# Transposes and gathers of the first experts moved between gate/up and down, with more PSUM banks

## The chip, the cores and the metric

One core of one Trainium2 chip runs the kernel. The metric is the time of one launch on the device in microseconds (us); a kernel's time is the median of its runs. All data are float32.

## The reference, cut to what matters

One step of a hybrid diffusion backbone: 128 context tokens and 256 latent tokens of width 2048 pass a mixer (attention and a long convolution), then a mixture of 16 SwiGLU experts. Only the experts matter here:

```python
aff = softmax(xs @ w_router)
g, idx = top_k(aff.T, cap)              # cap: 16 context and 32 latent tokens for each expert
xe = xs[idx]                            # gather
a, u = xe @ w_exp_gate, xe @ w_exp_up   # 2048 -> 1024 each
ye = (silu(a) * u) @ w_exp_down * g     # 1024 -> 2048
out = zeros.at[idx].add(ye)             # scatter
```

## The kernel before, in words

**The ring of weights.** Each expert reads 24 pieces of 1024 KB: 16 of gate and up (alternately, each with two channel tiles of 128), then 8 of down. They go through eight places of SBUF (`pieces`), loaded by SyncE's queue (lines 344 to 350). A place is asked for again when TensorE has released the piece in it (`piece_used`): gate/up pieces in pairs after each of the first seven iterations, down pieces one by one. The last two down pieces are asked for when gate/up is over (`gu_done`). The first piece of the next expert needs the first down piece of this one to be used.

**TensorE, one expert** (`expert`, line 818). Eight iterations `i` of gate/up wait for two pieces each and do eight matmuls of 48 slots by 512 columns (line 849; float32 shows two records for a matmul, so 16 in the trace). Then ScalarE takes the SiLU (line 1144), VectorE the product (line 1696), in two halves `n`; TensorE transposes each half (lines 869 to 871), VectorE copies it to `hTe` (line 1700), and eight steps `k` of down follow (line 898), ended by ScalarE's copies to `ye` (line 1148). Every second expert (2, 4, ...) also scatters the pair before it (line 815) beside gate/up and in the gap before down, into banks 4 to 6, which VectorE adds to `facc` (line 1691, semaphore `e_acc`).

**Gathering.** The gather is a matmul with a one-hot selection. For experts 0 to 5, `gather(k)` runs inside expert 0, one channel tile `k` ahead of its use. For experts 6 to 15, `gather_rest(k)` (lines 782 to 791: two matmuls of 320 columns and one of 160, all in bank 7) runs once in each of the eight iterations of experts 1 (`k` 0 to 7) and 3 (`k` 8 to 15). ScalarE copies each tile out of PSUM with the modulation (`gathered_rest`, lines 1119 to 1125, semaphore `gat2_a`). With one bank, tile `k` waits for the copy of tile `k-1`. In ScalarE's program these eight copies come ahead of the expert's two SiLUs.

**Scatter matrices.** `scatter_matrices(t)` (line 797) transposes eight tiles of `selG` for token tile `t` into banks 5 and 6; ScalarE copies them to `scat` (line 1130, semaphore `sg_cp`). All three run in expert 1, after the gathers of iterations 3, 5 and 6. GpSimd copies the inputs of the next expert (`next_inputs`, line 1216) at the end of gate/up, and after expert 1's the first scatter matrix, and clears `facc`.

The order on every engine is written out by hand; nothing is planned at build time.

Of the kernel before, what the change touches and what calls it, by code (L numbers as in the profile page):

```python
# [19 lines left out]
ACT = mybir.ActivationFunctionType  # L20
# [3 lines left out]
P = 128  # L24
D = 2048
KT = D // P
# [12 lines left out]
NE = 16  # L39
# [29 lines left out]
def paired(k):  # L69

    return slice(2 * P * (k // 2) + k % 2, 2 * P * (k // 2 + 1), 2)


def build(nc, x_prompt, x_sample, cache_k, cache_v, cols, w_ada, w_in, qk_g, w_attn_o, f1_w, f_vec, f2_w,
# [3 lines left out]
    with ctx:  # L78
# [286 lines left out]
        def _(pe):  # L365
# [416 lines left out]
            def gather_rest(k):  # L782

                if k == 0:
                    pe.wait_ge(sel2_ready, 3)
                else:
                    pe.wait_ge(gat2_a, k)
                kk, n = paired(k), NE2 * CAPL
                for t in range(2):
                    mm(bank(7, n), res[:, 1 + t, kk], selL[:, t, NE1:NE, :], start=t == 0, stop=t == 1)  # L790
                mm(bank(7, NE2 * CAPC, n), res[:, 0, kk], sel2C, start=True, stop=True).then_inc(gat2, 1)

            pe.wait_ge(sel_ready, 3)
            gather(0)
# [2 lines left out]
            def scatter_matrices(t):  # L797

                for n in (2 * t, 2 * t + 1):
                    pe.wait_ge(sg_ready, t + 1)  # L800
                    if n >= 2:
                        pe.wait_ge(sg_cp, n - 1)
                    for j in range(4):
                        last = trp(bank(5 + n % 2, P, j * P), selG[:, t, n % 2 * 4 + j, :], ident)
                    last.then_inc(sg_tr, 1)

            def scatter(pair, i, m, t):
# [10 lines left out]
            def expert(e, pair=None, first=False, final=False, rest=None):  # L818

                def beside(t):  # L820
                    if pair is not None:
                        scatter(pair, t // MT, t % MT, t)
                    if final and t < 4:
                        broadcast_gates(2 * t, 2, ones2, diag2_ready, g2_bc, g2_used)

                def landing(q):
                    pe.wait_ge(piece_in[q % 8], e * 48 + 16 * (q // 8 + 1))

                if not first:
                    pe.wait_ge(xe_st, e)  # L830
                if pair is not None:
                    pe.wait_ge(sc_st, pair + 1)
                if final:

                    pe.wait_ge(e_yc, 2 * e)
                for i in range(KT // 2):

                    landing(2 * i)
                    landing(2 * i + 1)
                    for k in range(2):  # L840
                        kk = 2 * i + k
                        if first:
                            if kk + 2 < KT:
                                gather(kk + 2)
                            pe.wait_ge(gat_lv, kk + 1)
                            pe.wait_ge(gat_ca, kk + 1)
                        for n in range(2):
                            for u in range(2):
                                last = mm(bank(n, p0=64 * u, p1=64 * u + SLOTS),  # L849
                                          xeT[:, kk, 0, :] if first else x_cur[:, kk, :],  # L850
                                          pieces[:, (2 * i + u) % 8, k * FF + n * NC_:k * FF + (n + 1) * NC_],
                                          start=kk == 0, stop=kk == KT - 1)
                            if kk == KT - 1:
                                last.then_inc(gu_done, 1)
                    if i < KT // 2 - 1:
                        last.then_inc(piece_used, 2)
                    if i % 2 == 1:
                        beside(i // 2)
                    if rest is not None:
                        gather_rest(rest + i)  # L860
                        if rest == 0 and i in (3, 5, 6):
                            scatter_matrices((3, 5, 6).index(i))
                if final:
                    pe.wait_ge(g2_used, 8)
                beside(4)
                for n in range(2):
                    pe.wait_ge(e_h, e * 2 + (n + 1))
                    for j in range(4):
                        o, src, i_ = bank(2 + n, SLOTS, j * SLOTS), h_s[0:SLOTS, n, j * P:(j + 1) * P], \
                            ident[0:SLOTS, 0:SLOTS]  # L870
                        last = mm(o, src, i_, start=True, stop=True) if j == 0 else trp(o, src, i_)
                    last.then_inc(e_htr, 1)
                beside(5)
                pe.wait_ge(e_hT, e * 2 + 1)
                if final:
                    for i in range(2):
                        for q in range(4):
                            landing(16 + 4 * i + q)
                            if i == 0 and q == 2:
                                pe.wait_ge(e_hT, e * 2 + 2)  # L880
                            if i == 1 and q == 2:

                                pe.wait_ge(sc_st, NE // 2)
                                for m in range(MT):
                                    scatter(NE // 2 - 1, 0, m, m)
                            for k in range(2):
                                for u in range(2):
                                    last = mm(bank(2 + i, p0=64 * u, p1=64 * u + SLOTS), hTe[:, 2 * q + k, :],
                                              pieces[:, 4 * i + q, k * FF + u * NC_:k * FF + (u + 1) * NC_],
                                              start=q == 0 and k == 0, stop=q == 3 and k == 1)  # L890
                        last.then_inc(down_done, 1)
                    return
                pe.wait_ge(e_hT, e * 2 + 2)
                for k in range(HK):
                    landing(16 + k)
                    for i in range(2):
                        for u in range(2):
                            last = mm(bank(2 + i, p0=64 * u, p1=64 * u + SLOTS), hTe[:, k, :],  # L898
                                      pieces[:, k, (2 * i + u) * NC_:(2 * i + u + 1) * NC_],
                                      start=k == 0, stop=k == HK - 1)  # L900
                        if k == HK - 1:
                            last.then_inc(down_done, 1)
                    if k < HK - 1:
                        last.then_inc(piece_used, 1)
# [2 lines left out]
            expert(1, rest=0)  # L907
            expert(2, pair=0)
            expert(3, rest=8)
            with pe.Fori(2, NE // 2 - 1) as p:  # L910
                expert(p * 2, pair=p - 1)
                expert(p * 2 + 1)
# [7 lines left out]
        def _(act):  # L920
# [197 lines left out]

            def gathered_rest(k):
                act.wait_ge(gat2, k + 1)  # L1120
                A(xeT[:, k, NE1:NE, 0:CAPL], bank(7, NE2 * CAPL).rearrange("p (e s) -> p e s", e=NE2),
                  ACT.Identity, bias=mod[:, SHIFT2 * KT + k, 1:2], scale=amp[:, 1, k, 1:2])
                A(xeT[:, k, NE1:NE, CAPL:SLOTS],
                  bank(7, NE2 * CAPC, NE2 * CAPL).rearrange("p (e s) -> p e s", e=NE2),
                  ACT.Identity, bias=mod[:, SHIFT2 * KT + k, 0:1], scale=amp[:, 1, k, 0:1]).then_inc(gat2_a, 1)

            def scatter_matrices(t):
                for n in (2 * t, 2 * t + 1):
                    act.wait_ge(sg_tr, n + 1)
                    A(scat[:, n % 2 * 4:n % 2 * 4 + 4, t * P:(t + 1) * P],  # L1130
                      bank(5 + n % 2).rearrange("p (j t) -> p j t", j=4), ACT.Copy).then_inc(sg_cp, 1)

            def expert(e, odd, rest=None):
                if rest is not None:
                    for i in range(8):
                        gathered_rest(rest + i)
                        if rest == 0 and i in (3, 5, 6):
                            scatter_matrices((3, 5, 6).index(i))
                for n in range(2):
                    act.wait_ge(gu_done, e * 2 + (n + 1))  # L1140

                    if n:
                        act.wait_ge(e_h, e * 2 + 1)
                    A(act_s[0:SLOTS, :], bank(n, p1=SLOTS), ACT.Silu).then_inc(e_silu, 1)  # L1144
                for i in range(2):
                    act.wait_ge(down_done, e * 2 + (i + 1))
                    for u in range(2):
# [4 lines left out]
            for k in range(KT):  # L1152
                gathered(k)
            act.wait_ge(ye_zero, 1)
            expert(0, 0)
            expert(1, 1, rest=0)
            expert(2, 0)
            expert(3, 1, rest=8)
# [697 lines left out]
```

## Time and profile before

| what | us |
|---|---|
| median of 3 runs | 2590.87 (2588.39 to 2595.32) |
| the profiled execution, whole | 2595.64 |
| its span, first to last instruction | 2593.7 |
| TensorE busy | 2409.6 (93%) |
| VectorE, ScalarE busy | 436.9, 236.9 |

The experts begin at 1596 us of the span: expert 0's down at 1644, expert 1's at 1710, expert 2's at 1771, expert 3's at 1831; the last expert's gate/up ends at 2539.5. Ahead of 1596 lie the mixer and the routing, which the change doesn't touch. Idle time of an engine costs nothing where another sets the pace, so the stretches are to be read one by one, with the DMA's rate beside TensorE's.

### The profile page before, as it was taken

To read this page: it belongs to the slowest core of one execution; us is meant where nothing else is said; L and a number is where in the kernel's file an instruction comes from. 1 tells how busy PE (TensorE), PEld (TensorE's weight loads), DVE (VectorE), ACT (ScalarE), POOL (GpSimd) and SP (SyncE) were. 2 spreads that over 40 slices of the span, in tenths; PEclk is the share of its full clock that TensorE was granted. 3 is DMA by queue.
4 is the path that set the end of the run, shared out by engine and by line. 5 is a ranking of instruction groups with operands and counts; after the bars stand their busy time and mean duration, and the time that the engine had idled before them with its cause. 6 is when DMAs were issued, how large, how long until landed. Compare 5 with 4: busy or idle time off the path is not lost.

```text
span 2593.7 us, 22327 instructions
## 1 busy us (share of the span) xinstructions
PE 2409.6 (93%) x8986; PEld 1132.3 (44%) x8986; DVE 436.9 (17%) x942; ACT 236.9 (9%) x486; POOL 46.0 (2%) x50
## 2 busy tenths in 40 slices
PE   5899999999999999999999997999989887979896
PEld 2355554444466666555554444333322222222222
DVE  4301111323122111000001204001011010101024
ACT  1100001000021111000000002111000000000001
POOL 0000000000000000000000000000000000000000
PEclk8899999999999999999999998999999999999998
DMA  9964454445423122524442223999999999999995
GB/s 362 352 235 167 174 189 155 147 157 198 162 65 98 65 98 76 200 101 159 162 162 99 97 97 136 388 386 415 416 421 422 422 422 422 422 422 421 422 421 209
DMA packets 196650, 644.87 MB, mean 249 GB/s; under 512 B 8423, under 2 KB 57992, under 8 KB 147112
## 3 DMA queue, kind: packets, MB, share of 16 engines
q1 hardware_dynamic: 194312, 635.55, 63.3%
q10 hardware_dynamic: 2208, 8.24, 0.9%
q8 instruction: 51, 0.84, 0.1%
q0 software_dynamic: 64, 0.13, 0.0%
q14 instruction: 15, 0.12, 0.0%
HBM read 640.21 MB, written 3.67 MB: 248 GB/s over the span
## 4 chain that ended last, share of the span: by engine, by line
PE 76%; DMA 19%; DVE 2%; ACT 1%; issue 1%; SPq 1%; DVEq 0%; ACTq 0%; POOL 0%; POOLq 0%
DMA ring<-in_w_up 14%; PE PS L652 13%; PE PS L404 10%; PE PS L419 10%; PE PS L849 8%; PE PS L898 7%; PE PS L687 6%; PE PS L746 6%; PE PS L671 3%; PE PS L378 3%; DMA ring<-in_w_down 2%; DMA ring<-in_w_ada 2%; PE PS L815 1%; PE PS L642 1%; PE PS L790 1%
## 5 line engine op out<-in xcount | busy, mean ns | idle before, releaser
L849 PE MATMUL PS<-ring,RF 128*48 128x512 f32 x1920 | 442.3, 605 | 77.1 <-DMA ring<-in_w_up 75.3
L652 PE MATMUL PS<-RB,ring 128*128 128x384 f32 x1024 | 336.2, 487 | 0.6 <-ACT RE L1047 0.6
L849 PEld LDWEIGHTS PS<-ring,RF 128*48 128x48 f32 x1920 | 132.3, 124 | 372.2 <-issue 371.7
L652 PEld LDWEIGHTS PS<-RB,ring 128*128 128x128 f32 x1024 | 193.9, 190 | 137.9 <-issue 3.4
L404 PE MATMUL PS<-RB,ring 128*128 128x384 f32 x768 | 251.2, 490 | 1.9 <-DMA ring<-in_w_in 1.9
L419 PE MATMUL PS<-ring,RB 128*128 128x512 f32 x576 | 252.4, 593 | 0.0
L898 PE MATMUL PS<-ring,RF 128*48 128x512 f32 x960 | 223.0, 622 | 6.9 <-DVE RF L1700 4.7
L404 PEld LDWEIGHTS PS<-RB,ring 128*128 128x128 f32 x768 | 146.4, 191 | 109.0 <-issue 9.6
L746 PE MATMUL PS<-ring,RC 128*128 128x512 f32 x384 | 169.2, 601 | 5.2 <-DVE RE L1573 4.7
L419 PEld LDWEIGHTS PS<-ring,RB 128*128 128x128 f32 x576 | 108.1, 190 | 132.1 <-issue 131.8
L898 PEld LDWEIGHTS PS<-ring,RF 128*48 128x48 f32 x960 | 64.2, 129 | 161.3 <-issue 149.0
L1691 DVE TENSOR_TENSOR RC<-RC,PS 128x512 f32<-128x512 f32 x96 | 64.3, 685 | 387.7 <-PE PS L815 387.5
L687 PE MATMUL PS<-RE,ring 128*128 128x384 f32 x384 | 126.5, 486 | 0.0
L746 PEld LDWEIGHTS PS<-ring,RC 128*128 128x128 f32 x384 | 73.7, 193 | 97.9 <-issue 97.3
L378 PE MATMUL PS<-ring,RG 128*32 128x512 f32 x768 | 92.9, 626 | 10.3 <-DMA ring<-in_w_ada 10.3
L815 PE MATMUL PS<-RB,RF 112*128 112x512 f32 x192 | 97.3, 632 | 4.3 <-DVE RC L1691 3.0
L687 PEld LDWEIGHTS PS<-RE,ring 128*128 128x128 f32 x384 | 73.0, 190 | 50.9
L1696 DVE TENSOR_TENSOR RG<-RF,PS 48x512 f32<-48x512 f32 x32 | 22.1, 690 | 389.8 <-ACT RF L1144 389.5
L671 PE MATMUL PS<-RE,ring 128*128 128x384 f32 x256 | 85.2, 486 | 0.0
L1347 DVE SCALAR_TENSOR_TENSOR RE<-PS,KC,RE 128x127 f32 (+1 forms) x96 | 35.5, 412 | 247.3 <-ACT RE L971 242.9
L1144 ACT ACTIVATE RF<-PS 48x512 f32<-48x512 f32 x32 | 18.9, 591 | 509.2 <-PE PS L849 472.8
L1148 ACT ACTIVATE RB<-PS 48x512 f32<-48x512 f32 x64 | 37.9, 592 | 280.3 <-PE PS L898 256.4
(241 smaller groups left out, 1313.7 us busy)
## 6 DMA issues: line engine op xcount, KB each, us to landing
ring<-in_w_gate SPq DMA_DIRECT2D x128, 1024.0 KB, 12.3
ring<-in_w_up SPq DMA_DIRECT2D x128, 1024.0 KB, 14.0
ring<-in_w_down SPq DMA_DIRECT2D x128, 1024.0 KB, 13.4
ring<-in_w_ada SPq DMA_DIRECT2D x48, 2048.0 KB, 13.2
ring<-in_w_in SPq DMA_DIRECT2D x40, 2048.0 KB, 8.1
ring<-in_w_attn_o SPq DMA_DIRECT2D x8, 2048.0 KB, 8.3
ring<-in_w_out SPq DMA_DIRECT2D x8, 2048.0 KB, 8.6
ring<-in_w_hy_o SPq DMA_DIRECT2D x4, 2048.0 KB, 8.0
```

The source lines that it names most:

```text
L378: last = mm(bank(rows_bank, p0=32 * g, p1=32 * g + 32), condS[:, kk, :], ring[:, j0 + h, k, :], start=kk < 4, stop=kk >= KT - 4)
L404: last = mm(bank(c, T), ring[:, 2 + h, k, c * P:(c + 1) * P], hT[:, h * HK + k, :], start=(h == 0 and k == 0), stop=(h == 1 and k == HK - 1))
L419: last = mm(bank(b0 + m), lhs[:, h * HK + k, m * P:(m + 1) * P], ring[:, (n + h) % 4, k, :], start=(h == 0 and k == 0), stop=(h == 1 and k ...
L652: last = mm(bank(F0, T), wide[:, n % 4, k, t % 2 * P:(t % 2 + 1) * P], hT[:, k, :], start=k == 0, stop=k == KT - 1)
L671: last = mm(bank(F1, T), ring[:, (n + 2) % 4, k, j * P:(j + 1) * P], hyT[:, k, :], start=k == 0, stop=k == HYT - 1)
L687: last = mm(bank(F1, T), wide[:, pa % 4, k, j % 2 * P:(j % 2 + 1) * P], qN[k // 4][:, k % 4, :, :].rearrange("p m d -> p (m d)"), start=k ...
L746: last = mm(bank(3 * (q % 2) + m), mixT[:, h * HK + k, m * P:(m + 1) * P], ring[:, n % 4, k, :], start=(h == 0 and k == 0), stop=(h == 1 a ...
L815: mm(bank(4 + n % 3), s_cur[0:64 + SLOTS, m * P:(m + 1) * P], ye[0:64 + SLOTS, 2 * i + u, :], start=True, stop=True).then_inc(e_sc, 1)
L849: last = mm(bank(n, p0=64 * u, p1=64 * u + SLOTS), xeT[:, kk, 0, :] if first else x_cur[:, kk, :], pieces[:, (2 * i + u) % 8, k * FF + n * ...
L898: last = mm(bank(2 + i, p0=64 * u, p1=64 * u + SLOTS), hTe[:, k, :], pieces[:, k, (2 * i + u) * NC_:(2 * i + u + 1) * NC_], start=k == 0, ...
L1148: last = A(ye[64 * odd:64 * odd + SLOTS, 2 * i + u, :], bank(2 + i, p0=64 * u, p1=64 * u + SLOTS), ACT.Copy)
L1691: tt(facc[:, m, q], facc[:, m, q], bank(4 + n % 3), ALU.add).then_inc(e_acc, 1)
```

## The change: what it does

- The transposes of the three `scatter_matrices` move from expert 1's gate/up to expert 0, between its gate/up and its down: one ahead of the transposes of each half `n`, one behind the last. Their eight-tile groups go through four banks (4 to 7) and no longer two. ScalarE copies them after expert 0's SiLUs.
- `gather_rest` of experts 1 and 3 does five tiles in the iterations 0 to 4; the other three are done between gate/up and down, at the same three places. It uses banks 6 and 7 in turn, and waits for the copy of the tile before the last.
- ScalarE does the SiLUs after five copies, and the last three copies behind them.
- Waits are added: tile 0 for the scatter matrices' copies, tile 8 for the accumulations of the first pair (its bank 6), and one for all gathers ahead of the loop over the later experts.

```diff
@@ gather_rest
                 if k == 0:
                     pe.wait_ge(sel2_ready, 3)
-                else:
-                    pe.wait_ge(gat2_a, k)
-                kk, n = paired(k), NE2 * CAPL
+                    pe.wait_ge(sg_cp, 2 * MT)
+                elif k == 8:
+                    pe.wait_ge(e_acc, 3 + 12)
+                    pe.wait_ge(gat2_a, k - 1)
+                elif k > 1:
+                    pe.wait_ge(gat2_a, k - 1)
+                b, kk, n = 6 + k % 2, paired(k), NE2 * CAPL
                 for t in range(2):
-                    mm(bank(7, n), ...)
-                mm(bank(7, NE2 * CAPC, n), ...).then_inc(gat2, 1)
+                    mm(bank(b, n), ...)
+                mm(bank(b, NE2 * CAPC, n), ...).then_inc(gat2, 1)
@@ scatter_matrices, TensorE
-                    if n >= 2:
-                        pe.wait_ge(sg_cp, n - 1)
+                    if n >= 4:
+                        pe.wait_ge(sg_cp, n - 3)
                     for j in range(4):
-                        last = trp(bank(5 + n % 2, P, j * P), ...)
+                        last = trp(bank(4 + n % 4, P, j * P), ...)
@@ expert, TensorE
+                    if rest is not None and i < 5:
+                        gather_rest(rest + i)
+
+                def between(j):
+                    if first:
+                        scatter_matrices(j)
                     if rest is not None:
-                        gather_rest(rest + i)
-                        if rest == 0 and i in (3, 5, 6):
-                            scatter_matrices((3, 5, 6).index(i))
+                        gather_rest(rest + 5 + j)
+
                 beside(4)
+                between(0)
                 for n in range(2):
                     pe.wait_ge(e_h, e * 2 + (n + 1))
                     ...
                     last.then_inc(e_htr, 1)
+                    between(1 + n)
@@ the experts, TensorE
             expert(3, rest=8)
+            pe.wait_ge(gat2_a, KT)
@@ expert, ScalarE
                 if rest is not None:
-                    for i in range(8):
+                    for i in range(5):
                         gathered_rest(rest + i)
-                        if rest == 0 and i in (3, 5, 6):
-                            scatter_matrices((3, 5, 6).index(i))
                 for n in range(2):
                     ...
                     A(act_s[0:SLOTS, :], bank(n, p1=SLOTS), ACT.Silu).then_inc(e_silu, 1)
+                if first:
+                    for t in range(MT):
+                        scatter_matrices(t)
+                if rest is not None:
+                    for i in range(5, 8):
+                        gathered_rest(rest + i)
```

## Rows read from the trace of the kernel before

**Rows 1.** The page's costliest groups: busy us, mean ns, idle before it, its releaser.
```profile
L849 PE MATMUL PS<-ring,RF 128*48 128x512 f32 x1920 | 442.3, 605 | 77.1 <-DMA ring<-in_w_up 75.3
```
**Rows 2.** Stretches (us from the span's start); the last columns are clock, DMA share, GB/s.
```profile
1644.00:1661.00 17.00, 16.95 (x66) 5.38 (x68) 0.00 (x0) 0.90 (x2) 0.00 (x0) 0.82 0.93 351
...
1710.00:1726.00 16.00, 16.00 (x64) 4.88 (x64) 0.00 (x0) 0.59 (x1) 0.00 (x0) 0.85 0.74 281
...
1770.00:1785.00 15.00, 15.00 (x63) 4.20 (x64) 0.86 (x2) 0.14 (x1) 0.51 (x1) 0.90 0.97 392
...
1832.00:1847.00 15.00, 15.00 (x68) 4.79 (x66) 0.00 (x0) 1.09 (x2) 0.00 (x0) 0.92 0.99 394
...
1860.00:2520.00 660.00, 570.23 (x2378) 180.57 (x2374) 73.94 (x132) 39.05 (x66) 12.37 (x18) 0.98 1.01 422
```
**Rows 3.** SyncE's issues of the first gate piece for experts 1 to 5, some second pieces.
```profile
1647.89 0.34 SPq L344 DMA_DIRECT2D ring<-in_w_gate  x1
1650.64 0.34 SPq L344 DMA_DIRECT2D ring<-in_w_up  x1
...
1713.68 0.33 SPq L344 DMA_DIRECT2D ring<-in_w_gate  x1
...
1773.86 0.33 SPq L344 DMA_DIRECT2D ring<-in_w_gate  x1
...
1834.90 0.33 SPq L344 DMA_DIRECT2D ring<-in_w_gate  x1
...
1892.41 0.33 SPq L344 DMA_DIRECT2D ring<-in_w_gate  x1
```
**Rows 4.** Timeline from gate/up's end to down, expert 0.
```profile
1634.16 5.36 PE L849 MATMUL PS<-ring,RE 128*48 128x512 f32 x24
...
1641.42 0.60 PE L871 MATMUL PS<-KC,RG 48*128 48x48 f32 x5 [1.90 <-DVE RG L1696]
...
1642.82 0.73 PE L871 MATMUL PS<-KC,RG 48*128 48x48 f32 x5 [0.80 <-DVE RG L1696]
...
1644.05 16.86 PE L898 MATMUL PS<-ring,RF 128*48 128x512 f32 x64 [0.49 <-DVE RF L1700]
```
**Rows 5.** The same, expert 1, from its last two iterations on.
```profile
1698.23 1.04 PE L804 MATMUL PS<-KC,RC 128*128 128x128 f32 x8
...
1699.20 3.64 PE L849 MATMUL PS<-ring,RF 128*48 128x512 f32 x16
...
1703.96 0.43 PE L791 MATMUL PS<-KC,RA 128*128 128x160 f32 x2
...
1709.83 16.40 PE L898 MATMUL PS<-ring,RF 128*48 128x512 f32 x64 [0.50 <-DVE RF L1700]
```
**Rows 6.** The same, expert 3.
```profile
1821.34 3.64 PE L849 MATMUL PS<-ring,RF 128*48 128x512 f32 x16
...
1831.32 15.39 PE L898 MATMUL PS<-ring,RF 128*48 128x512 f32 x64 [0.50 <-DVE RF L1700]
```
**Rows 7.** Last iterations of gate/up of experts 2, 4 and 5, downs of 4 and 5.
```profile
1758.92 3.64 PE L849 MATMUL PS<-ring,RF 128*48 128x512 f32 x16 [0.83 <-DMA ring<-in_w_up]
...
1879.12 3.64 PE L849 MATMUL PS<-ring,RF 128*48 128x512 f32 x16 [0.82 <-DMA ring<-in_w_up]
...
1890.29 4.93 PE L898 MATMUL PS<-ring,RF 128*48 128x512 f32 x22
...
1938.81 3.64 PE L849 MATMUL PS<-ring,RF 128*48 128x512 f32 x16 [1.33 <-DMA ring<-in_w_up]
...
1945.65 15.64 PE L898 MATMUL PS<-ring,RF 128*48 128x512 f32 x64 [0.64 <-DVE RF L1700]
```
**Rows 8.** TensorE alone: busy us (records), granted clock, DMA share, GB/s.
```profile
1571.00:1572.00 1.00, 0.06 (x1) 1.00 1.02 434
...
1645.00:1646.00 1.00, 1.00 (x6) 0.50 0.99 418
...
1891.00:1892.00 1.00, 1.00 (x6) 1.00 1.05 434
```

More of the change, by code:

```diff
@@ L785, in gather_rest @@
                     pe.wait_ge(sel2_ready, 3)
-                else:
-                    pe.wait_ge(gat2_a, k)
-                kk, n = paired(k), NE2 * CAPL
+                    pe.wait_ge(sg_cp, 2 * MT)
[5 more added lines that the diff above has]
+                b, kk, n = 6 + k % 2, paired(k), NE2 * CAPL
                 for t in range(2):
-                    mm(bank(7, n), res[:, 1 + t, kk], selL[:, t, NE1:NE, :], start=t == 0, stop=t == 1)
-                mm(bank(7, NE2 * CAPC, n), res[:, 0, kk], sel2C, start=True, stop=True).then_inc(gat2, 1)
+                    mm(bank(b, n), res[:, 1 + t, kk], selL[:, t, NE1:NE, :], start=t == 0, stop=t == 1)
+                mm(bank(b, NE2 * CAPC, n), res[:, 0, kk], sel2C, start=True, stop=True).then_inc(gat2, 1)
             pe.wait_ge(sel_ready, 3)
@@ L800, in scatter_matrices @@
                     pe.wait_ge(sg_ready, t + 1)
-                    if n >= 2:
-                        pe.wait_ge(sg_cp, n - 1)
+                    if n >= 4:
+                        pe.wait_ge(sg_cp, n - 3)
                     for j in range(4):
-                        last = trp(bank(5 + n % 2, P, j * P), selG[:, t, n % 2 * 4 + j, :], ident)
+                        last = trp(bank(4 + n % 4, P, j * P), selG[:, t, n % 2 * 4 + j, :], ident)
                     last.then_inc(sg_tr, 1)
@@ L1120, in gathered_rest @@
                 act.wait_ge(gat2, k + 1)
-                A(xeT[:, k, NE1:NE, 0:CAPL], bank(7, NE2 * CAPL).rearrange("p (e s) -> p e s", e=NE2),
+                A(xeT[:, k, NE1:NE, 0:CAPL], bank(6 + k % 2, NE2 * CAPL).rearrange("p (e s) -> p e s", e=NE2),
                   ACT.Identity, bias=mod[:, SHIFT2 * KT + k, 1:2], scale=amp[:, 1, k, 1:2])
                 A(xeT[:, k, NE1:NE, CAPL:SLOTS],
-                  bank(7, NE2 * CAPC, NE2 * CAPL).rearrange("p (e s) -> p e s", e=NE2),
+                  bank(6 + k % 2, NE2 * CAPC, NE2 * CAPL).rearrange("p (e s) -> p e s", e=NE2),
                   ACT.Identity, bias=mod[:, SHIFT2 * KT + k, 0:1], scale=amp[:, 1, k, 0:1]).then_inc(gat2_a, 1)
@@ L1130, in scatter_matrices, with expert @@
                     A(scat[:, n % 2 * 4:n % 2 * 4 + 4, t * P:(t + 1) * P],
-                      bank(5 + n % 2).rearrange("p (j t) -> p j t", j=4), ACT.Copy).then_inc(sg_cp, 1)
-            def expert(e, odd, rest=None):
+                      bank(4 + n % 4).rearrange("p (j t) -> p j t", j=4), ACT.Copy).then_inc(sg_cp, 1)
+            def expert(e, odd, first=False, rest=None):
                 if rest is not None:
-                    for i in range(8):
+                    for i in range(5):
                         gathered_rest(rest + i)
-                        if rest == 0 and i in (3, 5, 6):
-                            scatter_matrices((3, 5, 6).index(i))
                 for n in range(2):
@@ L1154, in _ @@
             act.wait_ge(ye_zero, 1)
-            expert(0, 0)
+            expert(0, 0, first=True)
             expert(1, 1, rest=0)
```

## The prediction

> **What bounds the kernel now.** I read the page's costliest groups first. The gate/up matmuls are the largest group, and their idle time, 77.1 us, was ended by a landing weight piece in 75.3 us of it [rows 1]. So TensorE is 93% busy and still waits for the DMA. Next I cut the experts into stretches [rows 2]. From 1860 to 2520 the DMA moves 422 GB/s without a break, and no stretch of the trace holds more for long: that is the rate at which the experts end. A piece of 1024 KB (1.049 MB) takes 1.049 / 422 = 2.485 us at it, an expert's 24 pieces 59.6 us. What can be gained in the experts is therefore only DMA time lost, not TensorE time. Lost time is the stretch times (1 - rate / 422) [rows 2]:
> - around expert 0's down, 17 x (1 - 351/422) = 2.9 us
> - around expert 1's down, 16 x (1 - 281/422) = 5.3 us, plus some 0.2 just ahead
> - around expert 2's down, 15 x (1 - 392/422) = 1.1 us
> - around expert 3's down, 15 x (1 - 394/422) = 1.0 us
>
> Together 10.5 us; nothing is lost after 1860. That is the ceiling. A loss comes when the first piece of the next expert, which needs the first down piece used, is asked for too late. I call "dry" the moment at which the pieces already asked for are all in. Expert 2's last gate/up pair had landed at 1758.92 [rows 7], eight more pieces are 19.9 us, so dry is 1778.8. Expert 3's first piece is asked for at 1773.86 [rows 3], 4.9 us ahead, and still 1.1 us goes in a thin queue. In expert 4 the last pair had landed at 1879.12 [rows 7], so dry is 1899.0; the next request comes at 1892.41 [rows 3], 6.6 us ahead, and nothing is lost [rows 2]. So about 6.5 us ahead of dry is enough, and each us of TensorE time ahead of the first down step counts only until that lead is reached.
>
> **The change, part by part.**
>
> Expert 0's gap. Gate/up ends at 1634.16 + 5.36 = 1639.5, down starts at 1644.05 [rows 4]. The transposes of one `scatter_matrices` take some 0.9 to 1.0 us (1698.23 to 1699.20, eight records) [rows 5]. The first fits into the idle 1.90 us ahead of 1641.42 [rows 4]. The half's transposes end at 1642.02; the second group ends near 1642.9, where the second half would start at 1642.82 anyway; then 0.7, then the third group 0.9: down starts near 1644.5, 0.45 late. The third group needs ScalarE's first two copies, which follow the second SiLU (about 1642.1) by 0.55 each, so they are there. What matters more is the clock: down ran its first steps at 1.2 GHz (clock 0.50) [rows 8] and took 16.86 us for 64 records, where 16 take 3.6 at 2.4 GHz, so 13.8 for 64. Expert 1's first piece was asked for 3.84 us after down's start (1647.89) and the second 2.75 later; at 2.4 GHz, expert 4's request came 2.1 us after down's start (1890.29 to 1892.41) [rows 3, 7, 8]. Does the fuller gap hold the clock? The nearest row for it: at 1571 TensorE idled some 0.9 us within a stretch of transposes and small matmuls, and the clock stayed 1.00 [rows 8]. The new gap has one idle us and is otherwise transposes. I take "held". Then the first request comes at 1644.5 + 2.1 = 1646.6, 1.3 earlier, and the 0.27 by which the second was slower than a piece's 2.485 go too. Of 2.9 us lost, 1.5 come back. Bounds: if the clock falls as before, the start is 0.45 to 1.2 us late (third group at twice its time), and that is lost.
>
> Expert 1. It now starts gate/up at 1644.5 + 13.8 = 1658.3 (before 1660.9). An iteration with a gather took 3.6 + 1.55 (gather from 1702.84 to 1704.39) [rows 5] = 5.13 us, against 4.97 for its two pieces; five are 25.7. The three left have 3.45 each: gate/up ends near 1694.4, the pieces being in (the last pair lands near 1689.5 counted from the earlier request). Before, it ended at 1702.84 [rows 5]: 8.4 us earlier, of which 2.6 from expert 0, 3.1 from two gathers less (the eighth lay behind the last matmuls already) and 2.7 from the transposes. The gap was 7.0 us, to 1709.83. The new one holds three gathers and two sets of five transposes: 3 x 1.4 + 2 x 0.65 = 5.5. Without any gather it would be 3.2 (expert 5, 1942.45 to 1945.65) [rows 7], so the SiLU and product chain is hidden: the first half's transposes wait for nothing once ScalarE's SiLU no longer stands behind the eighth tile's copies. The tile with `k` = 7 needs the copies of tile 5, which stand behind the second SiLU and end some 2.3 us into the gap; it comes at 4.2. Down starts at 1699.9, the next request at 1702, dry is near 1709.3: 7 us ahead. All 5.5 us come back. If the clock falls both times, down starts near 1703 and the request near 1706.5 with dry near 1711, and about 1 us stays lost: 4.4.
>
> Expert 2 does nothing new. Its gate/up is paced by landings [rows 7], so it stands to dry as before, and its 1.1 us stay (0, to 1.1 if its clock happens to hold as expert 4's does, clock 1.00 at 1891 [rows 8]). Expert 3 is nearly paced by the DMA: gate/up ended at 1824.98 [rows 6], and the last pair landed near 1819.7 (1778.8 + 1.1 + 16 x 2.485), so it can't end ahead of 1823.3. A gap of 5.4 gives down at 1828.7 instead of 1831.32 [rows 6], 2.6 us earlier, and the lead grows from 4.6 to 7.2 or more: 1.0 comes back (0.0 if the gathers run slow in the gap).
>
> The added waits. Tile 0 waits for the scatter copies; they end about 3.3 us after expert 0's second SiLU, near 1645.4, with expert 1's gathers at 1662. Tile 8 waits for the last sums of the first pair, made at expert 2's down, some 15 us ahead. The wait ahead of the loop is met during expert 3's down. Behind the scatter copies stand GpSimd's clearing of `facc` and VectorE's first sums; they now start with gate/up's end of expert 1 and are 8 us early. All are nothing, hidden under down, and a copy would have to be over 10 us late to cost. No DMA is moved; SyncE's order is the same. ScalarE's and VectorE's work is the same in sum, and neither is over 17% busy.
>
> **Sum.** 1.5 + 5.5 + 0 + 1.0 = 8.0 us off the profiled execution's 2595.64 (span 2593.7 and 1.94 around it): 2587.6. That execution is 4.8 above the median. Its first two downs took 16.86 and 16.40 us, later ones in a like gap 15.39 and 15.64 [rows 4 to 7]: they were 1 us slower than need be, so an average run may have lost 0.5 us less to begin with. I take 7.5 off the median: 2590.87 - 7.5 = 2583.4.
>
> **The rivals.**
> 1. **The clock falls in expert 0's gap all the same.** For it: the gap still has an idle us and small transposes, and in the trace down began at the low clock in experts 0, 1, 3 and 5, all longer than 13.8 us [rows 4 to 7]. Against it: the row at 1571. Then -0.8 + 4.6 + 0 + 1.0 = 4.8 off: 2586.1. The Trainium skill ("TensorE: Matmul & The Clock Gate", section "A second HAM failure mode: psum-queue depth-cycling") says that short idles between groups of matmuls, as banks are cycled, can make the clock swing between its levels. By that rule this rival holds and the sum is the one just given; the row at 1571 speaks against it.
> 2. **The loss has a floor.** In the trace some 1 us goes at each handover with a lead under 5 us. If the stretches of thin queue stay at experts 0, 1 and 3 with the leads of 7 us too, 1.0 + 4.5 + 0 + 0 = 5.5 off: 2585.4.
> 3. **Slower: the gaps run at 1.2 GHz from their start.** Everything between the products then takes twice as long. Expert 0: three groups of 1.8 and two sets of 1.2 put down at 1647.3, 3.3 late. Expert 1 ends gate/up at 1700.2 and has a gap of some 10.4: down at 1710.6, 0.8 later than before. Expert 3: 1823.3 + 10.4 = 1833.7, 2.4 later. Each us is DMA time lost: 3.2 us slower than before, 2594.1. It decides from the point where a gap is over some 8 us in expert 1 and 3. Against it: in expert 0's far emptier gap the second half's transposes still took 0.73 us where the first half's took 0.60 [rows 4], so there the clock was not yet halved.
> 4. **It does nothing, since the later experts would have made up the loss anyway.** 422 GB/s from 1860 on without slack speaks against it [rows 2]. 2590.9.
>
> **How the numbers follow.** Forecast (clock held in the gaps) 0.55, rival 1 0.22, rival 2 0.15, rival 3 0.04, rival 4 0.04. The forecast's own range is 6.5 to 9.6 off (with expert 2's loss gone): 2581.3 to 2584.4. A median of a few runs moves by 2 us (the three of before lie 7 apart). The range takes in rivals 1 and 2 with this: 2579.5 to 2588.5. A difference under 0.3% (7.8 us) can't well be told from none here. The forecast lies just inside that bound, so a bit under half of it, and with the scatter of the runs little of rivals 1 and 2, falls beyond: faster 0.40, same 0.57, slower 0.03.
>
> **What would show it.** In the changed kernel: down of expert 0 in 13.8 to 14.5 us with the clock at 1.00; expert 1's gate/up over near 1694 and down near 1700; its gap 5.5 us with no wait over 1 us in it; the DMA at 410 GB/s or more around expert 1's and 3's downs and near 385 around expert 0's; the last expert's gate/up 8 us earlier, at 2531.5. Wrong would make it: a slow clock at expert 0's down, a gap over 7 us in experts 1 or 3 (transposes waiting for ScalarE), or a rate under 400 around expert 1's down.

## The result and the profile after

The changed kernel takes 2584.45 us (median of 12 runs, 2583.56 to 2586.95), the one before 2590.41 in the same comparison (12 runs, 2586.12 to 2595.32): a ratio of 0.9979, with a 95% interval of 0.9971 to 0.9987. That is 6.0 us or 0.21% faster, where 7.5 was forecast. Two later comparisons gave 0.9978 (0.9968 to 0.9988) and 0.9968 (0.9956 to 0.9981), or 6.6 and 9.2 us by their medians. One of the changed kernel's seven runs in the last took 3767.63 us at a granted clock of 0.62; the ratio leaves it out, and it moves that median by less than 0.1 us.

The page's largest group of the changed kernel (busy us, mean ns, idle before it, its releaser) answers to [rows 1]:

```profile
L854 PE MATMUL PS<-ring,RF 128*48 128x512 f32 x1920 | 436.2, 595 | 94.8 <-DMA ring<-in_w_up 93.1
```

TensorE waits 17.8 us longer for pieces than before (93.1 against 75.3). It isn't slower for it: it now reaches the pieces earlier, which is how a kernel looks that has come nearer to its DMA bound.

Stretches of the changed kernel, columns as in [rows 2]; the first two answer to its rows of experts 0 and 1, the third to that around expert 3's down, and the last to the steady part:

```profile
1644.00:1661.00 17.00, 17.00 (x81) 5.08 (x80) 0.00 (x0) 3.11 (x6) 0.00 (x0) 1.00 0.98 387
...
1710.00:1726.00 16.00, 13.11 (x58) 4.05 (x54) 0.30 (x1) 2.36 (x4) 0.00 (x0) 1.00 1.01 421
...
1820.00:1835.00 15.00, 13.50 (x64) 3.89 (x60) 0.00 (x0) 2.93 (x6) 0.00 (x0) 1.00 1.01 420
1860.00:2520.00 660.00, 564.39 (x2378) 179.90 (x2379) 75.45 (x140) 39.05 (x66) 12.34 (x18) 0.98 1.01 422
```

The last column is what to read. Where expert 1's down lay before, the rate was 281 GB/s and is 421 (and it is 422 from 1700 to 1716, where that down lies now); around expert 0's it was 351 and is 387. The clock (third from the end) is 1.00 in the first three.

Expert 0's gap and down, in the timeline of TensorE and SyncE's queue (start, duration), which answer to [rows 3, 4]:

```profile
1638.91 1.09 PE L809 MATMUL PS<-KC,RC 128*128 128x128 f32 x8
...
1640.87 0.60 PE L883 MATMUL PS<-KC,RG 48*128 48x48 f32 x5 [0.87 <-DVE RG L1714]
...
1641.41 1.09 PE L809 MATMUL PS<-KC,RC 128*128 128x128 f32 x8
...
1642.43 0.60 PE L883 MATMUL PS<-KC,RG 48*128 48x48 f32 x5
...
1642.97 1.09 PE L809 MATMUL PS<-KC,RC 128*128 128x128 f32 x8
...
1643.99 13.94 PE L911 MATMUL PS<-ring,RF 128*48 128x512 f32 x64
1646.11 0.34 SPq L344 DMA_DIRECT2D ring<-in_w_gate  x1
```

and expert 1's, which answer to [rows 5]:

```profile
1691.12 3.64 PE L854 MATMUL PS<-ring,RF 128*48 128x512 f32 x16 [0.70 <-DMA ring<-in_w_up]
...
1694.69 1.35 PE L795 MATMUL PS<-RF,RA 128*128 128x320 f32 x4
...
1700.42 11.79 PE L911 MATMUL PS<-ring,RF 128*48 128x512 f32 x54
...
1702.55 0.33 SPq L344 DMA_DIRECT2D ring<-in_w_gate  x1
```

Expert 0's down takes 13.94 us, not 16.86, though it starts no earlier against gate/up's end (5.0 us behind it, before 4.5). Expert 1's starts 5.7 us after gate/up, not 7.0, and gate/up's last iteration now begins with a wait for a piece.

To compare kernels without what varies from run to run, three measures are used from here on, each from starts of rows in the timeline. **A** runs from expert 0's first gate/up matmul to the start of expert 2's last gate/up iteration, **B** from there to the last expert's last iteration, and the **tail** from there to the end of the span.

| kernel | start of A | A | B | tail |
|---|---|---|---|---|
| before | 1596.33 | 162.59 | 777.02 | 57.76 |
| before, second trace | 1600.10 | 161.87 | 776.68 | 54.55 |
| changed | 1595.79 | 154.89 | 776.69 | 54.53 |
| changed, second trace | 1595.98 | 154.88 | 776.71 | 54.53 |
| changed, third trace | 1596.30 | 154.87 | 776.92 | 56.21 |

The change lives in A: 7.7 us by the first traces, 7.0 by the second. B, in which experts 2 and 3 lost two us by their rates before, moves by 0.3 at most.

### The profile page after: what moved, and what is told of

Its sections match the earlier page's. It is cut to its first block, busy times and chain, and to the rows that moved or that the text cites. A ratio compares the mean times of both kernels' runs of the same rounds, so it can differ in the third digit from the quotient of the medians.

```text
span 2581.9 us, 22327 instructions
## 1 busy us (share of the span) xinstructions
PE 2392.4 (93%) x8986; PEld 1128.4 (44%) x8986; DVE 437.1 (17%) x942; ACT 237.2 (9%) x486; POOL 45.9 (2%) x50
## 4 chain that ended last, share of the span: by engine, by line
PE 75%; DMA 19%; DVE 2%; ACT 1%; issue 1%; SPq 1%; DVEq 0%; ACTq 0%; POOL 0%; POOLq 0%
DMA ring<-in_w_up 17%; PE PS L652 13%; PE PS L404 10%; PE PS L419 10%; PE PS L911 8%; PE PS L687 6%; PE PS L854 6%; PE PS L746 6%; PE PS L671 3%; PE PS L378 3%; DMA ring<-in_w_ada 2%; PE PS L820 1%; PE PS L642 1%; PE PS L466 1%; DVE RG L1714 1%
## 5 line engine op out<-in xcount | busy, mean ns | idle before, releaser
L854 PE MATMUL PS<-ring,RF 128*48 128x512 f32 x1920 | 436.2, 595 | 94.8 <-DMA ring<-in_w_up 93.1
L911 PE MATMUL PS<-ring,RF 128*48 128x512 f32 x960 | 217.8, 613 | 3.2 <-DVE RF L1718 3.2
```

What stands on the lines that cost most here:

```text
L854: last = mm(bank(n, p0=64 * u, p1=64 * u + SLOTS), xeT[:, kk, 0, :] if first else x_cur[:, kk, :], pieces[:, (2 * i + u) % 8, k * FF + n * ...
```

## The experiments

**Which part gives it.** First the scatter matrices alone, with the gathers of experts 1 and 3 back in the iterations (here and below TensorE's part of each edit; ScalarE's order follows it):

```diff
-                    if rest is not None and i < 5:
+                    if rest is not None:
                         gather_rest(rest + i)
...
-                    if rest is not None:
-                        gather_rest(rest + 5 + j)
```

> The changed kernel, but experts 1 and 3 do all eight gathers in their iterations again; the scatter matrices stay in expert 0's gap. Two measures from the trace: A is the time from expert 0's first gate/up matmul to the start of expert 2's last gate/up iteration (162.6 us before, 154.9 changed); B is from there to the last expert's last iteration (777.0 and 776.7). Theory 'what counts is when the next expert's first piece is asked for': expert 0 gives its 1.5 us as in the changed kernel; expert 1's gate/up ends near 1697, its gap is 7 us again and its clock falls, so the request comes near 1708 with the queue dry near 1711: 1.3 to 1.5 us lost, A = 156.3, time 2585.5 to 2586.5. Rival 'the gathers moved are the larger half': A = 159 or more, time 2588 or more.

Measured: A 156.95, B 777.27, tail 57.45; median 2588.74 (11 runs), ratio 0.9988 (0.9979 to 0.9997). Around expert 1's down (timeline):

```profile
1642.63 13.94 PE L908 MATMUL PS<-ring,RF 128*48 128x512 f32 x64
1644.75 0.34 SPq L344 DMA_DIRECT2D ring<-in_w_gate  x1
...
1702.87 15.96 PE L908 MATMUL PS<-ring,RF 128*48 128x512 f32 x64 [0.50 <-DVE RF L1712]
1706.72 0.33 SPq L344 DMA_DIRECT2D ring<-in_w_gate  x1
```

By A, this part alone brings 5.6 (or 4.9, against the second trace) of the 7.7 (7.0); 2.1 stay lost where 1.4 were expected. By A the request theory stands, a little under-priced. The time doesn't show it: 2588.74 is where the rival had put it (2588 or more) and not at 2585.5 to 2586.5. B and the tail of this trace are 0.6 and 2.9 us longer than the changed kernel's, which accounts for a part of that.

Then the gathers alone, with the scatter matrices' transposes back in expert 1's iterations (in two banks, 4 and 5):

```diff
                         gather_rest(rest + i)
+                    if rest == 0 and i in (3, 5, 6):
+                        scatter_matrices((3, 5, 6).index(i))
...
-                    if first:
-                        scatter_matrices(j)
```

> The changed kernel, but the scatter matrices' transposes are in expert 1's iterations again (behind iterations 3, 5 and 6, banks 4 and 5); the gathers stay split. By the request theory: expert 0 loses its 2.9 us as before (slow clock, down in 16 to 17 us), expert 1's gate/up ends near 1700.2, gap 5.6 at the full clock, request near 1708, dry near 1712.4: little more lost. A = 157.0 (156.5 to 157.5), time 2586 to 2587. Rival 'the two parts add up': each part gives half of the 7.7 us in A, so A = 158.5 to 159.

Measured: A 155.66, B 776.91, tail 56.22; 2586.47 (11 runs), ratio 0.9979 (0.9970 to 0.9988). Only 0.8 of A is missing, although expert 0's down ran slow again (15.63 us). That is less than both theories had (157.0 by the requests, within 156.5 to 157.5, and 158.5 or more by the rival). From 1644 to 1661 the rate is 364 GB/s, where it was 351 before and 387 in the changed kernel, and from 1700 to 1716 it is 421: nothing is lost at expert 1, and expert 0's part is worth 0.8 here, not the 1.5 that the first trace of before gave. 5.6 + 6.9 us alone, 7.7 together: the parts don't add up, since both aim at the same loss at expert 1's down, and either one cures most of it.

**The clock by itself.** The kernel before, with filling in the gaps of experts 0 and 1 and nothing moved:

```diff
                 beside(4)
+
+                def keep_busy():
+                    if first or rest == 0:
+                        for j in range(8):
+                            trp(bank(4, P, j % 4 * P), ident, ident)
+
+                keep_busy()
                 for n in range(2):
...
                     last.then_inc(e_htr, 1)
+                    keep_busy()
```

> The kernel before, with three groups of eight transposes of the identity (results unused) put into the gaps of experts 0 and 1, at the places where the changed kernel puts its work. Nothing is moved, so gate/up is as long as before. Theory 'half of the gain is the clock': downs of experts 0 and 1 in 13.9 us instead of 16.9 and 16.4, expert 0's handover gives 1.5, expert 1's request comes some 4 us earlier: A = 158.3 (157.5 to 159.3), time 2586.5 to 2588. Rival 'the gain is the shorter gate/up': A = 161.5 or more, time within 1 us of before.

Measured: A 158.23, B 777.09, tail 56.27; 2588.65 (11 runs), ratio 0.9985 (0.9976 to 0.9994).

```profile
1644.61 13.94 PE L906 MATMUL PS<-ring,RF 128*48 128x512 f32 x64
1646.73 0.34 SPq L344 DMA_DIRECT2D ring<-in_w_gate  x1
...
1707.56 13.94 PE L906 MATMUL PS<-ring,RF 128*48 128x512 f32 x64
1709.69 0.33 SPq L344 DMA_DIRECT2D ring<-in_w_gate  x1
```

Both downs run at full speed, and useless work in the gaps brings 3.6 to 4.4 us of A, over half of the whole. The median lies 0.65 us above the 2586.5 to 2588 that were expected. The rival, that only the shorter gate/up counts, is out.

**Expert 3.** The changed kernel, with expert 3's eight gathers in its iterations:

```diff
-                    if rest is not None and i < 5:
+                    if rest is not None and (i < 5 or rest == 8):
...
-                    if rest is not None:
+                    if rest == 0:
                         gather_rest(rest + 5 + j)
```

> The changed kernel, but expert 3 does its eight gathers in its iterations. A stays 154.9. Theory of the prediction 'expert 3's handover lost 1.0 us': B rises by 1.0, to 777.7. Rival 'with requests 4 to 5 us ahead of dry the rate dips only because the faster DMA queues run out ahead of the slowest, which costs nothing': B stays at 776.5 to 777.0 although the rate dips to some 380 GB/s for 10 us around 1825, and the time is that of the changed kernel within 0.5 us.

Measured: A 154.58, B 777.29, tail 54.53; 2583.33 (7 runs), ratio 0.9970 (0.9959 to 0.9981). The rate around expert 3's handover hardly dips (DMA share and GB/s at the end):

```profile
1822.00:1826.00 4.00, 4.00 (x16) 1.34 (x14) 0.00 (x0) 0.00 (x0) 0.00 (x0) 0.78 1.01 416
1826.00:1830.00 4.00, 4.00 (x20) 1.43 (x18) 0.00 (x0) 0.00 (x0) 0.00 (x0) 1.00 1.01 418
```

B is 0.4 to 0.6 over the changed kernel's three (776.69 to 776.92), between the two theories, and the time is none the longer. The edit brought hardly any of the dip back that it was to price. Other runs did: with the scatter matrices alone, where expert 3 gathers in its iterations too, the rate was 384 GB/s from 1825 to 1835, then 430 to 1845, and B 777.27. Over all runs with expert 3's gathers in its iterations, B is 776.68 to 777.29 (five traces, mean 777.07); over those with the work of experts 2 and 3 placed as in the changed kernel and nothing added there, 776.69 to 777.27 (seven traces, mean 776.90). So expert 3's part is worth 0.6 us at most, some 0.2 by the means, and no run here can tell it from nothing.

**Was the trace of before a typical one?** The second trace of the kernel before:

> The kernel before, unchanged, once more with a trace. In the four experiments so far A fell by 5.6, 6.9, 4.4 and 8.0 us against the trace of before, but the medians by 2.8, 5.1, 2.9 and 8.2. Theory 'the profiled execution of before had its slow-clock stretches at the worst places': A = 160.6 (159.5 to 161.5) and a tail (last expert's last iteration to the end) of 55 to 57 us instead of 57.8. Rival 'the medians hide something in the changed kernels': A = 162.6 within 0.3 again.

Measured: A 161.87, B 776.68, tail 54.55. The first two downs and the DMA around them:

```profile
1647.73 15.64 PE L898 MATMUL PS<-ring,RF 128*48 128x512 f32 x64 [0.50 <-DVE RF L1700]
...
1712.29 15.90 PE L898 MATMUL PS<-ring,RF 128*48 128x512 f32 x64 [0.50 <-DVE RF L1700]
```
```profile
1647.00:1664.00 17.00, 16.50 (x72) 6.00 (x72) 0.36 (x1) 1.42 (x3) 0.00 (x0) 0.90 0.95 369
1714.00:1730.00 16.00, 16.00 (x72) 5.17 (x70) 0.00 (x0) 2.36 (x4) 0.00 (x0) 0.93 0.81 300
```

The slow clock cost less here (15.64 and 15.90 us, not 16.86 and 16.40 [rows 4, 5]), and A is 0.7 shorter: the theory's direction, but a third of its size (160.6 was expected), and the rival's 162.3 to 162.9 didn't come either. The tail was as short as it ever is. At expert 2's handover there is no dip this time (416 to 423 GB/s from 1770 to 1785, where the first trace has 392), and B is only 0.3 shorter for it. Its median (8 runs, 2593.02) against another sample of the very same kernel in the same comparison (2591.55) shows how far such medians stray: 1.5 us.

And of the changed one:

> The changed kernel once more with a trace. Theory 'the gaps of experts 0, 1 and 3 hold the clock in every execution': A = 154.9 within 0.4, downs of experts 0, 1 and 3 in 13.9 to 14.0 us; what varies is the tail (54.5, or about 57.7 where the clock falls in the last expert's gap). Rival 'it held by luck': one of the three downs takes 15 us or more and A is 156 or more.

Measured: A 154.88, B 776.71, tail 54.53; downs of 13.94 in experts 0, 1 and 3; 2585.00 (8 runs). A and B repeat to 0.02 us between these two traces. The gaps hold the clock every time; in the third trace too (A 154.87), whose tail was 1.7 us longer and B 0.2:

> The changed kernel, as the yardstick for the three kernels sent with it: A = 154.9, B = 776.7, tail 54.5 (or 57.7), 2584.7 by its two medians so far.

Measured: 2582.32 (7 runs), tail 56.21.

**How early must the request come?** 36 transposes more at the end of the gaps of experts 1 and 3:

```diff
+                if rest is not None:
+                    for j in range(36):
+                        trp(bank(4, P, j % 4 * P), ident, ident)
                 beside(5)
```

> The changed kernel with 36 more transposes of the identity (results unused, about 4 us) at the end of the gaps of experts 1 and 3. The next expert's first piece is then asked for 4.4 us ahead of dry instead of 8.4. Theory of the prediction 'under 6.5 us ahead, about 1 us goes at each handover': A = 155.9, B = 777.7 and the time 2.0 us longer than the changed kernel's. Rival 'nothing is lost until the queue is really dry': A = 154.9 to 155.2, B within 0.3 of 776.7, time the same within 0.6, although the rate dips for some 10 us.

Measured: A 154.76, B 776.74, tail 56.24; 2586.07 (9 runs), ratio 0.9980 (0.9970 to 0.9990).

```profile
1691.55 3.64 PE L854 MATMUL PS<-ring,RF 128*48 128x512 f32 x16 [0.56 <-DMA ring<-in_w_up]
...
1700.76 4.09 PE L888 MATMUL PS<-KC 128*128 128x128 f32 x36
1704.78 13.94 PE L914 MATMUL PS<-ring,RF 128*48 128x512 f32 x64
1706.91 0.33 SPq L344 DMA_DIRECT2D ring<-in_w_gate  x1
```

Dry is 1691.55 + 19.9 = 1711.4, the request 4.5 us ahead of it, and neither A nor B loses anything. The prediction's threshold of 6.5 us was too high. (The median is 1.1 us over the changed kernel's in the same comparison, 2585.00, which the tail of 56.24 can account for.) With 60 transposes instead of 36:

> As the run with 36 further transposes at the ends of the gaps of experts 1 and 3 (A 154.8, B 776.7: nothing lost at 4.4 us ahead of dry), now with 60: some 6.8 us, the request 1.6 us ahead of dry. Theory 'a piece takes some us from request to a full rate, so a lead under about 3 costs': as expert 0's handover in the changed kernel (request 1.4 ahead, 1.4 us lost): A = 156.3, B = 778.0. Rival 'it costs only past dry': A within 0.3 of 154.9.

Measured: A 156.15, B 778.85, tail 54.54; 2590.82 (10 runs), ratio 0.9993 (0.9984 to 1.0002). 1.3 us are lost in A and 2.1 in B. In expert 3 the last pair landed at 1810.63, so dry is 1830.5; the request came at 1828.62, 1.9 us ahead:

```profile
1810.63 3.64 PE L854 MATMUL PS<-ring,RF 128*48 128x512 f32 x16 [1.34 <-DMA ring<-in_w_up]
...
1828.62 0.33 SPq L344 DMA_DIRECT2D ring<-in_w_gate  x1
```
```profile
1828.00:1830.00 2.00, 2.00 (x12) 0.56 (x10) 0.00 (x0) 0.00 (x0) 0.00 (x0) 1.00 0.70 205
1830.00:1832.00 2.00, 2.00 (x12) 0.61 (x10) 0.00 (x0) 0.00 (x0) 0.00 (x0) 1.00 0.87 336
1832.00:1834.00 2.00, 2.00 (x12) 0.65 (x10) 0.00 (x0) 0.00 (x0) 0.00 (x0) 1.00 0.83 295
1834.00:1836.00 2.00, 2.00 (x12) 0.55 (x10) 0.00 (x0) 0.00 (x0) 0.00 (x0) 1.00 0.93 356
```

In expert 1 the last pair had landed by 1689.0, so dry is 1708.9 at the latest and the request, at 1706.97, again 1.9 ahead of it at most. So the price starts between 4.5 and 1.9 us ahead of dry, and the theory of the run held (A 156.3 and B 778.0 were expected). Against 36 transposes, 2.6 us more work in each of two gaps ate about half of what the change brings, or more: 4.7 us of 6.0 by the medians, 3.5 of 7.0 to 8.0 by A and B. The traced run is the fastest of its ten, so what more the others lose isn't seen.

**Are the banks needed?** The changed kernel with the old banks (5 and 6 for the scatter matrices, 7 for the gathers):

```diff
-                    if n >= 4:
-                        pe.wait_ge(sg_cp, n - 3)
+                    if n >= 2:
+                        pe.wait_ge(sg_cp, n - 1)
                     for j in range(4):
-                        last = trp(bank(4 + n % 4, P, j * P), ...)
+                        last = trp(bank(5 + n % 2, P, j * P), ...)
```

> The changed kernel without its further banks: the scatter matrices go through banks 5 and 6 alone, the gathers through bank 7, each waiting for ScalarE's copy of the group before. Theory 'the gaps have room for these waits where the request is early': expert 0's down starts 0.65 us later and costs 0.5 of A, experts 1 and 3 start down 0.75 later, which costs nothing: A = 155.4, B = 776.7, time 0.5 us over the changed kernel's. Rival 'without the banks the gaps empty and the clock falls': a down of 15 us or more, A = 156.5 or more, 1.5 us or more slower than the changed kernel.

Measured: A 158.86, B 776.92, tail 56.14; 2587.01 (11 runs), ratio 0.9985 (0.9976 to 0.9994). Expert 0's gap:

```profile
1643.16 0.61 PE L879 MATMUL PS<-KC,RG 48*128 48x48 f32 x5 [0.87 <-DVE RG L1710]
1644.42 1.56 PE L805 MATMUL PS<-KC,RC 128*128 128x128 f32 x8 [0.65 <-ACT RB L1140]
1645.91 0.98 PE L879 MATMUL PS<-KC,RG 48*128 48x48 f32 x5
1646.82 1.97 PE L805 MATMUL PS<-KC,RC 128*128 128x128 f32 x8
```

From the third group of four on, each waits for a copy of ScalarE. With 0.65 us more idle time the clock is 0.50 from 1645 on (five records take 0.98 us, not 0.60), the gap is 7.4 us instead of 5.0, and down takes 15.42. From 1648 to 1665 the rate is 294 GB/s, which by the rates is 5.2 us lost where the changed kernel loses 1.4. The rival won: 4.0 of A are lost by the banks alone, as much as filling the gaps had gained. In expert 1's gap the same run waits 0.55 us twice for ScalarE, and its down starts at the full clock all the same.

**A faster version?** The changed kernel with useless transposes at two more places where the clock had fallen on the path: while TensorE waits for the top-k, and in the last expert's gap (here the second, shorter form):

```diff
+            for j in range(60):
+                trp(bank(6, P, j % 4 * P), ident, ident)
             pe.wait_ge(v_ready, 1)
...
                 between(0)
+                fill(8)
...
                     between(1 + n)
+                    if n == 0:
+                        fill(4)
```

> The changed kernel with transposes of the identity (results unused) at two more places: 70 while TensorE waits for the top-k (line 767), and 10, 5 and 5 in the gap of the last expert. Theory 'where the clock falls on the path that sets the end, holding it is time': the first two gathers of expert 0 run at 2.4 GHz (1.2 us), and the tail is 54.5 in every execution instead of 54.5 to 57.7 (1.5 on average): 2.7 us faster than the changed kernel, 2581.7. Rival 'the start is hidden behind the pieces' landing and the tail behind VectorE': the same time as the changed kernel within 0.8.

Measured: start of A 1592.71, A 155.19, B 777.27, tail 55.53; 2583.31 (6 runs), ratio 0.9972 (0.9960 to 0.9984). The 2581.7 that were expected didn't come. The filling was too long: the last expert's down began 10.0 us after its last iteration, in the changed kernel 9.1.

> As the kernel with both fillings, but shorter: 60 transposes while TensorE waits for the top-k (they end before it does, where 70 ended 0.7 us late), and 8 and 4 in the last expert's gap (10, 5 and 5 put its down 1.0 us late). Theory: expert 0 starts 1.2 us earlier than in the changed kernel against the top-k's end, and the tail is 54.6 in the trace and in every run: 1.2 + 1.5 = 2.7 us faster than the changed kernel in the same call. Rival: the tail's clock falls in few runs of the changed kernel, and only the 1.2 us at the start come.

Measured: start 1591.92, A 154.71, B 776.88, tail 54.59; span 2578.1; median 2581.45 (5 runs), ratio to before 0.9963 (0.9950 to 0.9976), 2582.32 for the changed kernel in the same comparison. From the end of the top-k chain to expert 0's first matmul it takes 5.3 us (1586.61 to 1591.92), in the changed kernel 7.8 (1588.02 to 1595.79). The part at the start shows in the trace with more than its 1.2 us; the medians differ by 0.9 us, a third of the 2.7 expected and less than such medians stray, so that it beats the changed kernel isn't shown.

## Why the prediction was right, and where its steps were off

The forecast case came in the traces: the clock held in all the gaps, and the requests went out about when they were to. The time lies in the whole range, the sign holds, and the difference of 0.21% is under the 0.3% bound. By the time alone it isn't decided: 2584.45 lies just outside the case's own range (2581.3 to 2584.4), 1.05 us above the forecast and 0.95 below rival 2's time.

- **The bound.** Right. With 421 GB/s where 281 was, the end came earlier, and nothing of it was given back between 1860 and 2520.
- **Expert 0.** Down was forecast 5.0 us behind gate/up's end, measured 5.0; its length 13.8 us, measured 13.94; the request 2.1 behind down's start, measured 2.12; 1.5 of 2.9 us to come back: 387 GB/s over 17 us leave 1.4 lost. But the 2.9 are those of the one trace of before; with the gathers alone, this part was worth 0.8 of A.
- **Expert 1.** Gap forecast 5.5, measured 5.7; down near 1699.9, measured 1700.42; request near 1702, measured 1702.55. The last pair landed at 1691.12, though, not near 1689.5, so dry was 1711.0 and the lead 8.5 us, not 7.
- **These two together** were priced at 7.0: A moved by 7.7 and 7.0. With expert 0's part at 0.8, expert 1's is 6.9 or 6.2 where 5.5 were put. That A and B moved by 8.0 in the first traces, just as summed, is in part luck: what expert 3 didn't give came from A. Against the second trace of before they moved by 7.0.
- **Expert 3: the mis-sized term.** 1.0 us was put there; B moved by 0.3 and 0.0, and undoing the part cost 0.6 of B at most. The step that failed is "lost time is the stretch times (1 - rate / 422)", where the lead is 4 to 5 us, with its rule that 6.5 us ahead of dry are needed. At 4.5 us nothing was lost. A dip at a handover that comes 4 to 5 us early is mostly not lost time; behind the dips the rate stood above 422 for a while (425 from 1847 to 1860 before, 430 from 1835 to 1845 with the scatter matrices alone). That the faster DMA queues there merely run out ahead of the slowest would explain it; no run shows the single queues, so this stays argued. Where the lead was 1.9 us, rate and landing agreed in kind (2.1 us of B, 2.4 by the rates in the four slices of the run with 60 transposes).
- **From the trace to the median.** 0.5 us were taken off for an unlucky trace of before. The second trace says 0.7 in A. The tail is as large a term and was not in the sum: 54.5 to 57.8 us in one trace or another, by whether the clock falls in the last expert's gap, which the change doesn't touch. It is a part of the reason that the two spans differ by 11.8 us (8.0 in A and B, 3.2 in the tail, 0.5 ahead of the experts) where the medians differ by 6.0. The 7.0 of A and B by the second trace still leave 1 us open, within what the medians stray.
- **Rival 1**, the clock falling in expert 0's gap, didn't come in any of the changed kernel's three traces. It did with the old banks. The prediction named the idle us but not that four banks are what keeps it at one. Of the rule of the Trainium skill ("TensorE: Matmul & The Clock Gate", section "A second HAM failure mode: psum-queue depth-cycling") on short idles between groups of matmuls, as banks are cycled, the traces say: with four banks it doesn't bite, and with two it did, in the one trace of that run.
- **Rival 2**, a floor of 1 us at every handover, is refuted by the 421 GB/s around expert 1's down and by the 36 transposes. **Rival 3** lacked its premise, as the gaps ran at the full clock. **Rival 4** fell with B.
- A rule was missed. The Trainium skill ("TensorE: Matmul & The Clock Gate", section "Part 4: PE-mode transpose") says that the full clock doesn't engage for transposes, which don't count as busy in the same way. By it the transposes in expert 0's gap could not have held the clock. Here it differs from the measurement, and the measurement decides: TensorE did nothing but transposes for 6.7 us in the run with 60 of them, from 1698.2 to 1704.9, and the clock (third column from the end) stayed full:

```profile
1700.00:1702.00 2.00, 2.00 (x20) 1.00 1.00 418
1702.00:1704.00 2.00, 2.00 (x21) 1.00 1.01 422
1704.00:1706.00 2.00, 2.00 (x15) 1.00 1.01 422
```

Transposes alone raised it too. In the trace of the shorter fillings the clock fell at 1577, behind a wait of 2.35 us. From 1578.0 to 1586.0 TensorE did the 60 added transposes and nothing else, and in them the clock came back:

```profile
1579.00:1580.00 1.00, 1.00 (x7) 0.50 0.00 0
1580.00:1581.00 1.00, 1.00 (x8) 0.71 0.00 0
1581.00:1582.00 1.00, 1.00 (x11) 1.00 0.00 0
```

## What to carry to other kernels

Where the DMA sets the pace through a ring of buffers, price an edit by one date: when the first request of the next round goes out, against when the queue runs dry. Here, moving that date earlier was worth its time up to a lead somewhere between 1.9 and 4.5 us, and nothing beyond. A gap on TensorE in front of that request costs twice, by its length and by the slow clock in the step that frees the buffer; filling it with moved work helps only if the fill itself doesn't wait, which is what the further banks buy. Compare traces by stretches between fixed rows: A of the changed kernel repeated to 0.02 us in three traces and B to 0.2, where its three medians lay 2.7 apart.

## What was unexpected of the hardware

- Float32 transposes held TensorE's clock at 2.4 GHz: 36 in 4.09 us, 60 in 6.71 us, and 24 among ten small ones in expert 0's 5.0 us. A stretch of 60 brought it back from 1.2 GHz.
- Small idle times decided the clock in expert 0's gap: with 0.87 us ahead of the first half's transposes it held in every trace, and with a further wait of 0.65 us it fell to 0.50. That is no measure for other gaps: with filling in the kernel before, expert 1's gap held it through an idle of 1.41 us (1.00 from 1704 to 1708). What idle is too much, no run here shows.
- The dips in the DMA's rate at experts 2 and 3 before (392 and 394 GB/s over 15 us each) were 0.3 us of time or less, not the 2.1 that the rate suggests.
